# One-core hybrid decoder layer: five waits and small stages moved inside the head turn

## The chip, the cores and the metric

One core of one Trainium2 chip runs the whole kernel in one launch. The metric is device time in microseconds, the median of the timed runs; lower is better. A separate, profiled execution gives the trace from which all rows below are copied. Engines in the rows: PE is TensorE's matmuls, PEld its weight loads, DVE is VectorE, ACT is ScalarE, POOL is GpSimd, SP the engine whose queue starts the DMAs.

## The reference, cut to what matters

A decoder layer on 512 tokens of width 1024. The change lies in the first part, in which eight attention heads and eight heads of a gated delta rule run side by side from one input projection.

```python
h = rmsnorm(x, attn_norm[i])
proj = h @ w_in[i]
qa, ka, va, qb, kb, vb, zb, bb, ab, gl = jnp.split(proj, cuts, axis=-1)
...
# attention head: softmax pairs, w = probs0 - lam * probs1, oa = w @ va
oa = (rmsnorm(oa, subln_a[i]) * (1.0 - lam_init))
...
# delta head: short convolution and silu, then unit norm of q and k
qkv = jax.nn.silu(causal_dwconv(jnp.concatenate([qb, kb, vb], axis=-1), conv_b[i]))
qb = l2norm(qb) * (DK_B ** -0.5)
kb = l2norm(kb)
...
def step(state, inp):                     # once for each chunk
    v_new = u_c - w_c @ state
    o = (q_c * jnp.exp(g_c)[..., None]) @ state + a_c @ v_new
    state = state * jnp.exp(g_last)[..., None, None] + jnp.swapaxes(k_dec, -1, -2) @ v_new
    return state, o
...
ob = rmsnorm(ob, onorm_b[i]) * jax.nn.silu(zb)
```

After it come the branch gates and projections, an output projection, a gated MLP with a convolution, and a gated per-layer embedding. The change touches none of these.

## The kernel before, in words

Every engine has a program of its own, written out by hand. An engine runs its instructions in the order in which they stand, and `wait_ge` on a semaphore holds it and all that is queued behind. Sequences lie along the free axis: a head's tensor is 128 x 512 (`T`), cut into four chunks of 128 tokens (`NT`).

**Projections.** Each projection is one 128-column slice of the weights times the normalized input: eight steps of three matmuls of 512 columns (line 488: high by high, high by low part, low part by high) into one of banks 0 to 3. SP loads a slice into one of four slots, POOL rounds it (`w_hi`, line 438) and makes the remainder (`w_lo`, line 424, four pieces), and PE multiplies.

**Turns.** The function `turn(h, ...)` exists once for each engine. Turn h computes the delta rule of head h, the attention and the convolutions of head a = h + 1, and projects what is needed next: in turns 0 to 5 the seven slices qb, kb, vb, zb, qa, ka, va. Turn -1 has no delta rule, turn 6 (`STEPS_LATE`) has four slices to project, and turn 7 has no attention. The changed places lie in turns -1 to 6. On PE the projection steps (`f.step(n)`) are dealt out between the small matmuls of the chain, to cover its waits; how many go where stands in `STEPS`.

**Levels.** For n = 1 to 6, PE multiplies (line 668), ACT copies the result to `ui` (1036), PE multiplies again (678, 680), and DVE updates `xi` and `xt` (1435, 1437); `make_ct` (1370) prepares the masked matrix `ct` of the next level. Side work rides along: `maxima(a, 3)` (1308, 1313) for the softmax; `decay_beta` (1392), which multiplies `dec` by the beta rows that lie in bank 6; `finish_silu` (1354). `b_sum` (609) on PE sums the squares of q, then of k, into bank 6, which `decay_beta` must have read before; `b_r` on ACT (Ln at 867, Exp at 868) turns each sum into a norm. Its Ln signals `b_ln`: bank 6 has been read.

**Scan.** For chunk t = 0 to 3: a product with the state (724) and the state part of the output into bank 6 (726), from t = 1 on; DVE's copy of `us` (1479, 1483, semaphore `vnew`); the state's increment into bank 5 (735, `kv`); the output's second part into bank 6 (736); and DVE's update of `state` (1489, 1491). Around t = 0 stands `attend` (599), which makes head a's output in bank 3. ACT squares it (1080, `oa_sq`) and PE sums the squares into bank 4 (744, `oa_sum`), from which comes the output's norm. ACT's `silu_exp(a, 2)` (992, 967, 968) is the sigmoid of the convolved v (`b_sigmoid2`). `gate_z` (1001, 1006, 967, 968) copies z out of its bank and makes its sigmoid (`z_sigmoid`); DVE multiplies the two in `finish_z` (1515). DVE's side work in the scan is a list from which two entries are taken at each t: one after the copy of `us`, one after the update of the state.

Of the kernel before, what the change touches and what calls it, by code (L numbers as in the profile page):

```python
# [156 lines left out]
def build(nc, x, p, w_in, attn_norm, qnorm_a, knorm_a, lam_a, subln_a, rel_bias, conv_b, a_log_b,  # L157
# [4 lines left out]
    with ctx:  # L162
# [5 lines left out]
        def sem(name):  # L168
            if name not in sems:
                sems[name] = ctx.enter_context(nc.semaphore(name))  # L170
            return sems[name]
# [61 lines left out]
        qb, kb, vb, zb = (sb(n, [P, T], F32, ws) for n in ("qb", "kb", "vb", "zb"))  # L233
# [238 lines left out]
        def _(pe):  # L472
# [147 lines left out]
            def turn(h, at, fill, delta=True, attention=True, more_a=True, steps=STEPS):  # L620

                a = h + 1
# [96 lines left out]
                for t in range(NT):  # L719
                    ts = slice(t * P, (t + 1) * P)  # L720
                    if delta and t > 0:
                        pe.wait_ge(sem("state"), h * 3 + t)

                        pe.matmul(tiles(7)[:, t, :], wt_[:, t, :], state[:, :], start=False, stop=True,
                                  skip_group_check=True).then_inc(sem("ws"), 1)
                        pe.matmul(bank[6][:, ts], state[:, :], qeg[:, t, :], start=True, stop=False, skip_group_check=True)
                    f.step(scan[1 + t][0])
                    if delta:
                        pe.wait_ge(sem("vnew"), h * NT + (t + 1))
                        if t == 0:  # L730
                            pe.wait_ge(sem("w_copied"), h + 1)
                            if attention:
                                pe.wait_ge(sem("b_ln"), a * 2 + 2)
                        if t < NT - 1:
                            pe.matmul(bank[5][:, 0:P], kdec[:, t, :], us[:, t, :], start=True, stop=True).then_inc(sem("kv"), 1)
                        mm = pe.matmul(bank[6][:, ts], us[:, t, :], at_[:, t, :], start=(t == 0), stop=True, skip_group_check=True)
                        if t == NT - 1:
                            mm.then_inc(sem("ob_mm"), 1)
                    f.step(scan[1 + t][1])
                    if t == 0 and attention:  # L740
                        attend(a)
                    if t == 1 and attention:
                        pe.wait_ge(sem("oa_sq"), a + 1)
                        pe.matmul(bank[4][:, :], ones, pr[1][:, :], start=True, stop=True).then_inc(sem("oa_sum"), 1)  # L744
                for n, name in enumerate(("qa", "ka")):
# [110 lines left out]
        def _(act):  # L856
# [3 lines left out]
            def done(ins, name, value):  # L860

                ins.then_inc(sem(name) if isinstance(name, str) else name, 1)
                act.wait_ge(sem(name) if isinstance(name, str) else name, value)
# [89 lines left out]
            def keep_w(h, i):  # L953
                act.wait_ge(sem("a_turned"), h * 4 + (i + 1) + 1)
                done(nc.scalar.activation(wT[:, 0:i + 1, i * P:(i + 1) * P], tiles(3)[:, 0:i + 1, :], ACT.Copy),  # L955
                     "a_wT", h * 4 + (i + 1))
# [60 lines left out]
            def turn(h, at, delta=True, attention=True, more_a=True):  # L1017

                a = h + 1
                if not attention:  # L1020

                    act.wait_ge(sem("oa_done"), H + 1)
                    for k in range(H):
                        done(nc.scalar.activation(oa_hi[:, k, :], o_a[:, k, :], ACT.Copy), "o_high", k + 1)
                if attention:
                    softmax(a, 0)
                if h > 0:
                    ob_r(h - 1)
                if attention:
                    keep_w(a, 0)  # L1030
                    first_tap(a, 0, at("qb"))
                    softmax(a, 1)
                for n in range(1, NL):
                    if delta:
                        act.wait_ge(sem("level_u"), h * (NL - 1) + n)
                        done(nc.scalar.activation(ui[:, :, :], tiles(7), ACT.Copy), "ui", h * (NL - 1) + n)  # L1036
                    if attention:
                        if n == 2:
                            keep_w(a, 1)
                            silu_exp(a, 0)  # L1040
                        if n == 3:
                            softmax(a, 2)
                            first_tap(a, 1, at("kb"))
                            act.wait_ge(sem("g_rows"), a + 1)
                            if delta:
                                act.wait_ge(sem("qeg"), h + 1)
                            nc.scalar.activation(egl[:, a % 2, :, :], tiles(6)[:, :, P - 1:P], ACT.Exp)
                            done(nc.scalar.activation(eg[:, :, :].rearrange("p t c -> p (t c)"), bank[6][:, :], ACT.Exp),
                                 "eg", a + 1)
                            square_b(a, 0)  # L1050
                        if n == 4:
                            act.wait_ge(sem("g_rows_read"), a + 1)
                            done(nc.scalar.activation(dec[:, :, :], dec[:, :, :], ACT.Exp), "dec", a + 1)
                            keep_w(a, 2)
                        if n == 5:
                            silu_exp(a, 1)
                            softmax(a, 3)
                            b_r(a, 0)
                        if n == 6:
                            square_b(a, 1)  # L1060
                            first_tap(a, 2, at("vb"))
                    if n in (1, 3) and not attention:
                        gate_a(n // 2)
                    if n == 2 and not attention:
                        gate_z(h, at("zb"), attention)
                if delta:
                    act.wait_ge(sem("w_mm"), h + 1)
                    done(nc.scalar.activation(wt_[:, :, :], tiles(5), ACT.Copy, scale=-1.0), "w_copied", h + 1)
                if not attention:
                    gate_a(2)  # L1070
                    gate_a(3)
                if attention:
                    keep_w(a, 3)
                    v_copy(a)
                    b_r(a, 1)
                    if delta and more_a:
                        gate_z(h, at("zb"), attention)
                    silu_exp(a, 2)
                    act.wait_ge(sem("a_out"), a + 1)
                    done(nc.scalar.activation(pr[1][:, :], bank[3][:, :], ACT.Square), "oa_sq", a + 1)  # L1080
                    if more_a:
                        prep_qk(h + 2, 0, at("qa"))
                    act.wait_ge(sem("oa_sum"), a + 1)
                    rsqrt(pr[1][:, :], bank[4][:, :], 1.0 / P, ("oa_ln", "oa_r"), a + 1)
                    if not more_a:
                        gate_z(h, at("zb"), attention)
                if more_a:
                    prep_r(h + 2, 0, at("qa"))
                    prep_qk(h + 2, 1, at("ka"))
                if delta:  # L1090
                    act.wait_ge(sem("ob_mm"), h + 1)
                    if h > 0:
                        act.wait_ge(sem("ob_done"), h + 1)
                    done(nc.scalar.activation(sqo[:, :], bank[6][:, :], ACT.Square), "ob_sq", h + 1)
                if more_a:
                    prep_r(h + 2, 1, at("ka"))
                    prep_v(h + 2, at("va"))
# [11 lines left out]
            def b_r(h, n):  # L1109
                act.wait_ge(sem("b_sum"), h * 2 + (n + 1))  # L1110
                rsqrt(sqb[n][:, :], bank[6][:, :], 1.0, ("b_ln", "b_r"), h * 2 + (n + 1))
# [90 lines left out]
        def _(dve):  # L1202
# [195 lines left out]
            def turn(h, at, delta=True, attention=True, more_a=True):  # L1398

                a = h + 1  # L1400
# [27 lines left out]
                for n in range(1, NL):  # L1428
# [27 lines left out]
                    if n == 4 and attention:  # L1456
                        steps(conv(a, 1, at("kb")))
                        maxima(a, 3)
                    if n == 5 and attention:
                        decay_beta(a)  # L1460
                        steps(finish_silu(a, 1))
                        combine(a, 3)
                    if n == 6 and attention:
# [6 lines left out]
                side = []  # L1470
                if attention:
                    side = conv(a, 2, at("vb")) + [lambda: scale_qk(a, 1)]
                if delta and (more_a or not attention):
                    side = side + [lambda: finish_z(h)]
                if attention:
                    side = side + finish_silu(a, 2)
                if delta:
                    dve.wait_ge(sem("u_mm"), h + 1)
                    done(V.tensor_copy(us[:, 0, :], tiles(7)[:, 0, :]), "vnew", h * NT + 1)
# [221 lines left out]
```

## Time and profile before

| | |
|---|---|
| time, median of 3 | 1396.91 us (1396.87 to 1397.35) |
| the profiled execution's own time | 1394.66 us |
| its span, first to last instruction | 1392.6 us |
| mean granted TensorE clock in it | 0.99 |
| PE busy | 1305.9 us, 94% of the span |
| DVE, ACT, POOL busy | 724.6, 523.3, 642.4 us |
| PE waits for `oa_sq` at line 744, by the list of waits | 14.7 us, 7 times |
| PE waits for `decb` at line 609 | 9.5 us, 8 times |
| PE waits for `b_ln` at line 735 | 7.4 us, 7 times |

Busy shares are averages over the whole span. The change is about single waits, so the rows below follow one turn. A row of a timeline gives start, duration, engine, line, operation and tiles, the count of merged instructions, and in brackets the idle time of the engine just before with what ended it. A matmul's printed duration overlaps its successor's start: dense matmuls of 512 columns start 0.23 us apart though each is printed with 0.39 or 0.40.

### The profile page before, as it was taken

What the parts mean: (1) busy time and instruction counts of PE and PEld (TensorE: products, weight loads), DVE (VectorE), ACT (ScalarE), POOL (GpSimd) and SP (SyncE); (2) the same over time, 40 slices, a digit from 0 to 9 for tenths busy, and PEclk for the clock granted to TensorE, in tenths of its full rate; (3) what the DMA queues carried; (4) which work ended last, traced back from release to release, by engine and by line L of the source; (5) the groups of instructions that cost most, each with busy time, mean ns of one, the idle gap of its engine ahead of it and who ended that gap; (6) DMA issues with size and microseconds to landing.
All of it is one profiled execution on the core that took longest, in us unless ns stands there. A gap on an engine that the chain in (4) does not pass through costs nothing.

```text
span 1392.6 us, 19271 instructions
## 1 busy us (share of the span) xinstructions
PE 1305.9 (94%) x6453; PEld 1044.9 (75%) x6453; DVE 724.6 (52%) x1137; ACT 523.3 (38%) x811; POOL 642.4 (46%) x757
## 2 busy tenths in 40 slices
PE   4889999898999989899899999999999999999998
PEld 3657768676777867677688888877887778878776
DVE  3264748375473836547452113215888871781634
ACT  4353444435344453534423322345332221221252
POOL 2434243242424335242253646436666775666533
PEclk9999999999999999999999999999999999999999
DMA  6412111111111111111122335222333224233222
GB/s 187 120 46 60 32 49 43 46 50 42 47 45 46 46 37 55 46 46 31 34 63 56 106 88 168 76 76 76 105 91 91 87 87 127 60 91 110 68 75 80
DMA packets 188128, 100.71 MB, mean 72 GB/s; under 512 B 3654, under 2 KB 186905, under 8 KB 188057
## 3 DMA queue, kind: packets, MB, share of 16 engines
q1 hardware_dynamic: 188057, 99.79, 25.0%
q8 instruction: 41, 0.67, 0.2%
q14 instruction: 30, 0.25, 0.1%
HBM read 97.67 MB, written 2.11 MB: 72 GB/s over the span
## 4 chain that ended last, share of the span: by engine, by line
PE 51%; POOL 19%; issue 17%; DVE 6%; ACT 5%; SPq 1%; DMA 0%; POOLq 0%; DVEq 0%; ACTq 0%
PE bank L488 30%; POOL w_lo L424 19%; PE bank L680 3%; PE bank L668 3%; PE bank L678 2%; PE bank L585 1%; PE bank L609 1%; PE bank L599 1%; PE bank L565 1%; PE bank L744 1%; PE bank L631 1%; PE bank L592 1%; ACT pr L949 1%; DVE ast L1313 1%; PE bank L640 1%
## 5 line engine op out<-in xcount | busy, mean ns | idle before, releaser
L424 POOL TENSOR_TENSOR w_lo<-w_raw,w_hi 128x256 fp32r<-128x256 f32 x692 | 576.4, 867 | 302.1 <-ACT w_hi L876 297.2
L488 PE MATMUL bank<-hn_hi,w_hi 128*128 128x512 f32 x1000 | 423.5, 424 | 9.3 <-POOL w_lo L424 9.3
L488 PE MATMUL bank<-hn_hi,w_lo 128*128 128x512 f32 x1000 | 393.5, 394 | 0.0
L488 PE MATMUL bank<-hn_lo,w_hi 128*128 128x512 f32 x1000 | 392.6, 393 | 0.0
L438 POOL CAST w_hi<-w_raw 128x1024 fp32r<-128x1024 f32 x61 | 65.8, 1079 | 431.6 <-PE bank L488 431.6
L488 PEld LDWEIGHTS bank<-hn_hi,w_hi 128*128 128x128 f32 x1000 | 190.1, 190 | 54.7 <-issue 19.5
L488 PEld LDWEIGHTS bank<-hn_hi,w_lo 128*128 128x128 f32 x1000 | 189.2, 189 | 41.3
L488 PEld LDWEIGHTS bank<-hn_lo,w_hi 128*128 128x128 f32 x1000 | 190.3, 190 | 37.7 <-issue 6.7
L876 ACT ACTIVATE w_hi<-w_raw 128x1024 fp32r<-128x1024 f32 x120 | 127.4, 1062 | 109.3 <-PE bank L488 95.2
L1600 DVE SCALAR_TENSOR_TENSOR u<-vr,pt,u 128x511 f32<-128x511 f32 x88 | 75.1, 853 | 12.9 <-DVE u L1598 1.2
L1174 ACT ACTIVATE s<-u 128x512 f32<-128x512 f32 x22 | 13.9, 633 | 178.7 <-DVEq L1603 178.7
L488 PE MATMUL bank<-fa_hi,w_hi 128*128 128x512 f32 x176 | 71.3, 405 | 2.2 <-POOL w_lo L424 2.2
L488 PE MATMUL bank<-fa_hi,w_lo 128*128 128x512 f32 x176 | 68.6, 390 | 0.0
L488 PE MATMUL bank<-fa_lo,w_hi 128*128 128x512 f32 x176 | 68.6, 390 | 0.0
L1036 ACT ACTIVATE ui<-bank 128x512 f32<-128x512 f32 x48 | 28.8, 599 | 83.7 <-PE bank L668 83.0
L668 PEld LDWEIGHTS bank<-xi,ct 128*128 128x128 f32 x384 | 48.9, 194 | 9.9 <-issue 8.0
L668 PE MATMUL bank<-xi,ct 128*128 128x128 f32 x384 | 52.5, 280 | 0.9 <-DVE xi L1435 0.9
L1370 DVE TENSOR_TENSOR ct<-lt,sq 128x512 f32<-128x512 f32 x56 | 51.3, 916 | 2.8 <-DVE qb L1343 0.2
L680 PE MATMUL bank<-xt,ui 128*128 128x64 f32 x384 | 50.9, 275 | 0.0
L680 PEld LDWEIGHTS bank<-xt,ui 128*128 128x128 f32 x384 | 46.8, 192 | 1.9 <-ACT ui L1036 1.7
L678 PEld LDWEIGHTS bank<-ui,xt 128*128 128x128 f32 x320 | 40.9, 191 | 9.7 <-ACT ui L1036 7.3
L955 ACT ACTIVATE wT<-bank 128x128 f32<-128x128 f32 (+3 forms) x32 | 14.0, 438 | 87.1 <-PE bank L592 87.1
(259 smaller groups left out, 1882.8 us busy)
## 6 DMA issues: line engine op xcount, KB each, us to landing
w_raw<-in_w_in SPq DMA_DIRECT2D x73, 512.0 KB, 3.8
w_raw<-in_w_up SPq DMA_DIRECT2D x44, 512.0 KB, 3.8
w_raw<-in_w_down SPq DMA_DIRECT2D x16, 512.0 KB, 4.0
w_raw<-in_w_br_a SPq DMA_DIRECT2D x8, 512.0 KB, 4.1
w_raw<-in_w_br_b SPq DMA_DIRECT2D x8, 512.0 KB, 4.0
w_raw<-in_w_out SPq DMA_DIRECT2D x8, 512.0 KB, 4.0
w_raw<-in_w_ple_gate SPq DMA_DIRECT2D x8, 512.0 KB, 4.1
w_raw<-in_w_down SPq DMA_DIRECT2D x8, 384.0 KB, 3.4
```

The source lines that it names most:

```text
L424: ins = pool.tensor_tensor(wlo[c.slot][:, ks, :], raw[c.slot][:, ks, :], whi[c.slot][:, ks, :].bitcast(F32), ALU.subtract)
L438: pool.tensor_copy(whi[c.slot][:, :, :], raw[c.slot][:, :, :]).then_inc(high_ready, 1)
L488: mm = pe.matmul(acc, w[c.slot][:, i, :], xx[:, x0 + i, :], start=(i == 0 and n == 0), stop=last)
L565: pe.matmul(bank[c.bank][:, :], half, sqr[n][:, :], start=True, stop=True).then_inc(sem("a_sum"), 1)
L668: mm = pe.matmul(tiles(7)[:, t, :], ct[n % 2][:, t, :], xi[:, t, :], start=True, stop=True)
L678: pe.matmul(packed(5, n, 0, t), xt[:, t, :], lane(ui[:, t, :], n, 0), start=True, stop=True)
L680: mm = pe.matmul(packed(5, n, 1, t), ui[:, t, :], lane(xt[:, t, :], n, 1), start=True, stop=True)
L876: done(nc.scalar.activation(whi[c.slot][:, :, :], raw[c.slot][:, :, :], ACT.Copy), high_ready, c.number + 1)
L955: done(nc.scalar.activation(wT[:, 0:i + 1, i * P:(i + 1) * P], tiles(3)[:, 0:i + 1, :], ACT.Copy), "a_wT", h * 4 + (i + 1))
L1036: done(nc.scalar.activation(ui[:, :, :], tiles(7), ACT.Copy), "ui", h * (NL - 1) + n)
L1370: done(V.tensor_tensor(ct[n % 2][:, :, :], lt[:, :, :], level_mask(n), ALU.mult), "ct", h * NL + (n + 1))
L1600: link(V.scalar_tensor_tensor(out=u[:, back:], in0=vr[:, 0:T - back], scalar=tap(j), in1=u[:, back:], op0=ALU.mult, op1=ALU.add))
```

## The change

No operation is added or taken away, and no size changes. Six places are edited:

- PE, scan at t = 0: the wait for `b_ln` moves from ahead of the state's increment (735 before, 733 after) to behind it, where line 736 is the first to write bank 6.
- PE: the sum of squares of the attention output (744) moves from behind t = 1 to behind t = 2.
- ACT: `b_r(a, 1)`, k's norm, moves ahead of `keep_w(a, 3)` and `v_copy(a)`.
- ACT: `gate_z` moves from ahead of `silu_exp(a, 2)` to behind the square `oa_sq` (turns 0 to 5).
- DVE: `decay_beta(a)` moves from level 5 to level 4, behind `maxima(a, 3)`; in turns with a delta rule it thereby stands ahead of `make_ct` and the updates of level 5.
- DVE: `finish_silu(a, 2)` and `finish_z(h)` change places in the side list.

```diff
@@ PE, scan @@
                         if t == 0:
                             pe.wait_ge(sem("w_copied"), h + 1)
-                            if attention:
-                                pe.wait_ge(sem("b_ln"), a * 2 + 2)
                         if t < NT - 1:
                             pe.matmul(bank[5][:, 0:P], kdec[:, t, :], us[:, t, :], start=True, stop=True).then_inc(sem("kv"), 1)
+                        if t == 0 and attention:
+                            pe.wait_ge(sem("b_ln"), a * 2 + 2)
                         mm = pe.matmul(bank[6][:, ts], us[:, t, :], at_[:, t, :], start=(t == 0), stop=True, skip_group_check=True)
...
-                    if t == 1 and attention:
+                    if t == 2 and attention:
                         pe.wait_ge(sem("oa_sq"), a + 1)
                         pe.matmul(bank[4][:, :], ones, pr[1][:, :], start=True, stop=True).then_inc(sem("oa_sum"), 1)
@@ ACT @@
                 if attention:
+                    b_r(a, 1)
                     keep_w(a, 3)
                     v_copy(a)
-                    b_r(a, 1)
-                    if delta and more_a:
-                        gate_z(h, at("zb"), attention)
                     silu_exp(a, 2)
                     act.wait_ge(sem("a_out"), a + 1)
                     done(nc.scalar.activation(pr[1][:, :], bank[3][:, :], ACT.Square), "oa_sq", a + 1)
+                    if delta and more_a:
+                        gate_z(h, at("zb"), attention)
@@ DVE @@
                     if n == 4 and attention:
                         steps(conv(a, 1, at("kb")))
                         maxima(a, 3)
+                        decay_beta(a)
                     if n == 5 and attention:
-                        decay_beta(a)
                         steps(finish_silu(a, 1))
...
+                if attention:
+                    side = side + finish_silu(a, 2)
                 if delta and (more_a or not attention):
                     side = side + [lambda: finish_z(h)]
-                if attention:
-                    side = side + finish_silu(a, 2)
```

What stands on ACT behind the levels of turn 0 (`ui` is not shown; `silu0` takes v, `silu1` takes z; a - row is of before, a + row of after):

```order
+L867 ACTIVATE sqb1<-bank6,sm 128x512 [waits b_sum,w_copied]
+L868 ACTIVATE sqb1<-sqb1 128x512 [waits b_ln]
+L955 ACTIVATE wT<-bank3 128x4x128 [waits a_turned,b_r]
 L919 ACTIVATE va<-bank4 128x512 [waits va_T,a_wT]
-L867 ACTIVATE sqb1<-bank6,sm 128x512 [waits b_sum,va_ready]
-L868 ACTIVATE sqb1<-sqb1 128x512 [waits b_ln]
-L1001 ACTIVATE zb<-bank1 128x512 [waits product,b_r]
+L992 ACTIVATE silu0<-vb 128x512 [waits b_silu,b_conv2,va_ready]
+L967 ACTIVATE silu0<-silu0,sm 128x512 [waits scalar_step]
+L968 ACTIVATE silu0<-silu0 128x512 [waits scalar_step]
+L1078 ACTIVATE pr1<-bank3 128x512 [waits a_out,b_sigmoid2]
+L1001 ACTIVATE zb<-bank1 128x512 [waits product,oa_sq]
```

The norm now stands ahead of the two copies, and z's copy (its exponential, logarithm and exponential follow it) behind the square of the attention output, where before it stood ahead of v's sigmoid.

On DVE, in the same turn, the end of the side work in the scan, from chunk t = 2 on (`vbt` is the memory of `us`):

```order
 L1483 COPY vbt<-bank 128x128 [waits ws,qkb_ready]
-L1515 TENSOR_TENSOR zb<-zb,silu 128x512 [waits z_sigmoid,vnew]
-L1491 SCALAR_TENSOR_TENSOR state<-state,egl,bank 128x128 [waits kv,zb_ready]
-L1354 TENSOR_TENSOR vb<-vb,silu 128x512 [waits b_sigmoid2,state]
-L1483 COPY vbt<-bank 128x128 [waits ws,vb_ready]
+L1354 TENSOR_TENSOR vb<-vb,silu 128x512 [waits b_sigmoid2,vnew]
+L1491 SCALAR_TENSOR_TENSOR state<-state,egl,bank 128x128 [waits kv,vb_ready]
+L1515 TENSOR_TENSOR zb<-zb,silu 128x512 [waits z_sigmoid,state]
+L1483 COPY vbt<-bank 128x128 [waits ws,zb_ready]
 L1499 SCALAR_TENSOR_TENSOR o_a<-bank,sm,pr 128x512 [waits oa_r,vnew]
```

The product with z now stands directly ahead of the last copy of `us`, and v's product ahead of the last update of the state.

On DVE, levels 4 and 5 of the same turn:

```order
 L1313 TENSOR_REDUCE ast<-bank 128x1 [waits a_exp,vector_step]
 L1313 TENSOR_REDUCE ast<-bank 128x1
-L1370 TENSOR_TENSOR ct<-lt,sq 128x512 [waits a_nmax]
+L1392 TENSOR_TENSOR decb<-dec,bank 128x512 [waits b_rows,dec,a_nmax]
+L1370 TENSOR_TENSOR ct<-lt,sq 128x512 [waits decb]
 L1435 TENSOR_TENSOR xi<-xi,bank 128x8x32 [waits level_vt,ct]
 L1437 TENSOR_TENSOR xt<-xt,bank 128x8x32 [waits xi]
-L1392 TENSOR_TENSOR decb<-dec,bank 128x512 [waits b_rows,dec,xt]
-L1354 TENSOR_TENSOR kb<-kb,silu 128x512 [waits b_sigmoid1,decb]
+L1354 TENSOR_TENSOR kb<-kb,silu 128x512 [waits b_sigmoid1,xt]
```

`decb` now stands ahead of `ct` and of the two updates instead of behind them.

## Rows read from the trace of the kernel before

**Rows 1.** The page, its first line.

```profile
span 1392.6 us, 19271 instructions
```

**Rows 2.** Waits, whole span: who waited for whom, us in total, times, longest.

```profile
PE bank L744 <- ACT pr L1080: 14.7, 7, 2.7
...
PE bank L609 <- DVE decb L1392: 9.5, 8, 1.8
...
PE bank L735 <- ACT sqb L867: 7.4, 7, 1.1
```

**Rows 3.** Windows: stretch, us, each engine's busy time, granted clock, DMA share, GB/s.

```profile
244.89:326.16 81.27, 76.61 (x432) 60.66 (x433) 47.35 (x87) 36.68 (x68) 29.40 (x36) 1.00 0.17 46
326.16:409.05 82.89, 78.25 (x433) 61.60 (x433) 47.04 (x87) 36.69 (x68) 30.04 (x36) 0.98 0.17 45
...
346.40:349.90 3.50, 3.50 (x8) 2.30 (x9) 0.91 (x2) 0.00 (x0) 0.00 (x0) 0.51 0.02 5
```

**Rows 4.** Timeline of PE in turn 1, pieces from level 6 on.

```profile
243.16 0.39 PE L488 MATMUL bank<-hn_lo,w_hi 128*128 128x512 f32 x1
243.39 0.40 PE L488 MATMUL bank<-hn_hi,w_lo 128*128 128x512 f32 x1
244.89 1.10 PE L609 MATMUL bank<-sqb,sq 128*128 128x512 f32 x2 [1.10 <-DVE decb L1392]
...
257.32 0.46 PE L735 MATMUL bank<-vbt,kdec 128*128 128x128 f32 x2 [1.06 <-ACT sqb L867]
...
265.12 1.12 PE L744 MATMUL bank<-pr,sq 128*128 128x512 f32 x2 [2.00 <-ACT pr L1080]
266.08 0.39 PE L724 MATMUL bank<-state,ui 128*128 128x128 f32 x2
...
268.36 0.38 PE L724 MATMUL bank<-state,ui 128*128 128x128 f32 x2
...
269.50 0.38 PE L736 MATMUL bank<-at_,vbt 128*128 128x128 f32 x2
```

**Rows 5.** Timeline of ACT in the scan of turn 1.

```profile
257.87 0.60 ACT L1001 ACTIVATE zb<-bank 128x512 f32<-128x512 f32 x1
...
259.74 0.63 ACT L968 ACTIVATE silu<-silu 128x512 f32<-128x512 f32 x1
262.39 0.63 ACT L992 ACTIVATE silu<-vb 128x512 f32<-128x512 f32 x1 [2.02 <-DVEq L1345]
...
264.47 0.60 ACT L1080 ACTIVATE pr<-bank 128x512 f32<-128x512 f32 x1
```

**Rows 6.** Timeline of DVE in turn 1, levels 4 and 5, then the scan.

```profile
241.20 1.14 DVE L1370 TENSOR_TENSOR ct<-lt,sq 128x512 f32<-128x512 f32 x1
243.15 0.42 DVE L1435 TENSOR_TENSOR xi<-xi,bank 128x256 f32<-128x256 f32 x1 [0.81 <-PE bank L680]
...
244.06 0.69 DVE L1392 TENSOR_TENSOR decb<-dec,bank 128x512 f32<-128x512 f32 x1
...
266.90 0.69 DVE L1515 TENSOR_TENSOR zb<-zb,silu 128x512 f32<-128x512 f32 x1
...
268.85 0.29 DVE L1483 COPY vbt<-bank 128x128 f32<-128x128 f32 x1
```

**Rows 7.** Line 1515 over the whole run: durations in ns, min/median/max.

```profile
L1515 DVE TENSOR_TENSOR zb<-zb,silu x8: 691/692/1240, 185.7 to 739.8; 128x512 f32<-128x512 f32 x8
```

**Rows 8.** Timeline of POOL behind the scan of turn 1.

```profile
270.72 1.04 POOL L438 CAST w_hi<-w_raw 128x1024 fp32r<-128x1024 f32 x1 [11.97 <-PE bank L488]
```

**Rows 9.** Timeline of PE in turn 6.

```profile
653.28 1.65 PE L609 MATMUL bank<-sqb,sq 128*128 128x512 f32 x2 [1.85 <-DVE decb L1392]
...
672.96 1.12 PE L744 MATMUL bank<-pr,sq 128*128 128x512 f32 x2 [2.69 <-ACT pr L1080]
```

**Rows 10.** Windows of turn 6 behind those two waits, columns as in Rows 3.

```profile
653.28:657.10 3.82, 3.82 (x12) 2.87 (x13) 2.04 (x4) 1.68 (x3) 0.00 (x0) 0.55 0.02 4
...
672.96:678.49 5.53, 5.45 (x21) 4.26 (x22) 1.94 (x5) 1.32 (x2) 0.00 (x0) 0.69 0.00 0
```

## The prediction

> **What bounds the kernel now.** I read the list of waits first, then windows over single turns, then the timeline of each engine in one turn. In turn 1, from one sum of q's squares to the next, PE is busy 76.61 of 81.27 us [rows 3], so PE is the engine that sets the pace of a turn, and a turn gets shorter only by what PE stops waiting. The list of waits has three waits of PE that the change aims at: 14.7 us for the square of the attention output, 9.5 for `decb`, 7.4 for k's norm [rows 2]. In turn 1 they are 2.00, 1.10 and 1.06 us [rows 4]; turns 0 to 5 repeat these three within 0.01 us, and turn 6 has 2.69, 1.85 and 1.06 [rows 2, 9].
>
> The printed idle time is a little less than the loss. Dense matmuls start 0.23 us apart (243.16, 243.39), and line 609 starts 1.50 behind the last of them, so this wait costs 1.27 against 1.10 printed [rows 4]. I add the same 0.16 or so to the others: 1.22 for k's norm and 2.16 for the square. Together 4.65 us in a turn.
>
> The clock is a cost of its own. Behind the 2.00 us stall of turn 2 the granted clock was 0.51 in a window of 3.50 us, the lower of the two levels (1.2 against 2.4 GHz), and that turn took 82.89 us where turn 1 took 81.27: 1.62 us for one fall [rows 3]. Two of the six 2.00 us stalls were followed by a fall (turns 2 and 5), as were the 1.85 and 2.69 us stalls of turn 6 (granted 0.55 and 0.69 behind them, [rows 10]); none of the stalls of 1.0 to 1.1 us was.
>
> **Part by part, in a turn of 0 to 5, by the times of turn 1.** Nothing is added, so no work term appears; it is all order.
>
> *decay times beta, level 4.* `decb` takes 0.69 us and would run from 241.20 to 241.9, where `ct` started before [rows 6]. Its inputs are made earlier in the level, and PE has not asked for bank 6 by then. PE's line 609 then goes at 243.62: 1.27 saved. What becomes late is `ct` and with it `xi`: `ct` took 1.14 us, so it would end at about 243.1 instead of 242.3, and `xi` waits for PE until 243.15 anyway [rows 6]. Even 0.6 us of lateness in `xi` is covered, since the sum of squares occupies PE for 0.96 us (as line 744 does from 265.12 to 266.08, [rows 4]) between PE's arrival and the next level's product. I cost it at nothing; without that cover it would be up to 0.4.
>
> *k's norm.* ACT has been free since it copied `w`, and the sum was made long before the scan, so the Ln that frees bank 6 runs well before it is wanted; besides, the increment no longer waits for it. Saved: 1.22. The two copies that now stand behind the norm wait for PE's transposes anyway and keep their place.
>
> PE reaches the scan's first increment 1.27 + 1.22 = 2.49 earlier, at 254.83. The chain behind it (state, convolution of v, sigmoid of v, square) hangs on that increment: v's first exponential starts at 262.39 - 2.49 = 259.90 and the square is ready at 264.47 + 0.60 - 2.49 = 262.58 [rows 4, 5].
>
> *The sum, one chunk later.* PE would arrive at the old place 2.00 + 0.16 before the square. The new place is one chunk behind, which is 268.36 - 266.08 = 2.28 us of PE work [rows 4]. That is 0.12 more than the wait: the 2.16 are saved, with next to nothing to spare.
>
> *z's gate, and the new wait.* This is the one place where the change makes something late. `gate_z` took 257.87 to 260.37 = 2.50 us, in time that ACT had free; now it starts behind the square, at about 262.6, and ends at 265.12 [rows 5]. DVE's product with z (0.69) starts 0.1 behind that, and the last copy of `us` (0.29) is queued behind it: 265.2 + 0.69 + 0.03 + 0.29 = 266.2 [rows 6]. PE takes the result 0.15 later (`decb` ends at 244.75, line 609 starts at 244.89, [rows 4, 6]), so the last product with `us` (736) starts at 266.35. Without this wait PE would be there at 269.50 - 2.49 - 2.16 = 264.85 [rows 4]. **New stall: 1.50 us.** PE holds everything behind it, the projections too. The trace of before has no such wait. Its bounds: nothing if z were early after all, 2.05 if the product takes its longest 1.24 us [rows 7]. I take 1.50, since the product's median is 0.69 [rows 7] and each other part is a row too.
>
> Here the Trainium skill speaks against the change. Its page "SBUF — State Buffer", section "SBUF: two separate sides", says that VectorE and GpSimd share a port pair which one of them holds for a whole instruction, and that a VectorE operation with two SBUF inputs is among those that it blocks. The product with z has two such inputs, so by that rule the product waits wherever a GpSimd piece is under way.
>
> What the rows say of it: the product took between 0.69 and 1.24 us [rows 7]. With 1.24 in each of the six turns the sum would be 3.3 smaller and the time 1370.2. POOL stood idle 11.97 us before its cast at 270.72, thus through the scan from 258.75 on, waiting for PE [rows 8]; even moved 3 us earlier, that stretch covers the product, so I keep 0.69.
>
> *v's sigmoid before z.* It is ready at 264.44 - 2.49 = 261.95, its product and the state's update fit ahead of 263.7, when PE has finished line 744. Nothing.
>
> Net in a turn: 1.27 + 1.22 + 2.16 - 1.50 = 3.15; six turns 18.9.
>
> *Falls of the clock.* Turns 2 and 5 lose their fall at the square: 2 x 1.62 = 3.2. A stall of 1.50 is between those that never brought a fall (1.1) and those that did (1.85, and 2.00 in two of six); I take none.
>
> *Turn 6.* No z here in the scan. `decb`: 1.85 + 0.16, of which I take off 0.3, an estimate, since the next steps then meet ACT still busy with the softmax: 1.7. k's norm 1.2. The square: 2.69 + 0.16 = 2.85, but a chunk of this turn has one projection step fewer (three dense matmuls, 0.70), thus 2.28 - 0.70 = 1.58 of cover, so 1.27 stay: 1.6 saved. Two falls [rows 10]: 3.2. Together 7.7.
>
> *Turn -1.* It has no delta rule; `decb` stands where it stood relative to the other work, and PE waits about 0.2 for the square, which goes. 0.2.
>
> Sum: 18.9 + 3.2 + 7.7 + 0.2 = 30.0. The profiled execution's own time is 1394.66 (span 1392.6, [rows 1]), 2.25 below the median shown. So 1364.7 for a profiled execution, and 1366.9 for the median. The weights can follow: the POOL row shows that it waits for PE, not PE for it [rows 8].
>
> **Rivals.**
>
> *The new stall starts falls of the clock.* For it: 1.50 us is nearer to 1.85 than 1.06 is, and the stall follows other short pauses. Against: seven stalls of 1.06 and eight up to 1.85 brought one fall. Two to six falls cost 3.2 to 9.7: 1370 to 1377. Chance 0.14.
>
> *z costs nothing.* If ACT or PE were 1.5 us off in my favour, for instance if PE meets a further wait of its own in chunk 2 that z hides behind: six turns gain 1.50 more, 1357.9. Against: the z chain is 5.2 us of ACT behind v's convolution, and every part is a row [rows 5]. Chance 0.06.
>
> *A moved stage is late somewhere else.* The sum has 0.12 us to spare only, `xi` some 0.5. If another wait takes the place of the `decb` or of the square's wait (1 to 2 us in a turn), six turns give back 6 to 12: 1373 to 1379, 1382 at the worst. Chance 0.10.
>
> *POOL meets z's product.* Each product takes 1.24: 1370.2, as worked out above. Chance 0.04.
>
> *Hidden anyway.* If PE's lead is only spent waiting for weights, the time stays. Against: [rows 8], and no wait for weights shows in turns 0 to 5. 1396.9. Chance 0.02.
>
> *Slower: the z chain holds the scan.* The same place, line 736 at t = 3, behind ACT's gate and DVE's product. The stall must be longer than 1.50 + 30.0 / 6 = 6.5 us for the time to rise. That needs ACT to start the gate 5 us later than I have it, say behind a projection that is not finished. Before, `gate_z` ran at 257.87 without waiting for its projection, which speaks against it [rows 5]. At 8 us: 1396.9 + 6 x 1.5 = 1406. Chance 0.03.
>
> **How the numbers follow.** The forecast has 0.61, with its own range 1362 to 1371 (product with z at 1.24 in most turns: up to +3.3; 0.12 us of spare missed by 0.3: +1.8; new stall 1 us shorter in each turn: about -5). Adding z at no cost at the lower end and falls or another wait at the upper end, 1359 to 1377 leaves out less than 2 in 10. A time within 0.2% (2.8 us) of before is all that this kernel's measurement cannot tell from no change; of the cases only the hidden one ends there, 0.02 and 0.01 more for mixtures. Slower has 0.03, faster 0.94.
>
> **What the profile after would show.** PE's wait at line 609 for `decb`, at the first increment (then line 733) for ACT's norm, and at 744 for the square are gone in turns 0 to 5; 744 keeps about 1.1 in turn 6. A new wait of PE at line 736 for DVE's copy, 1.3 to 1.5 us printed, in each of turns 0 to 5, with DVE at 1515 waiting for ACT's 968. The turn from one line 609 to the next takes 78.1 us. Half-clock windows behind 744 are gone. Wrong would be: another releaser in front of 668 or 744, a stall at 736 over 2 us or absent, or falls behind it.

## The result and the profile after

The changed kernel takes 1364.62 us (median of 4, 1363.99 to 1365.4) against 1396.89 for the kernel before in the same runs: a ratio of 0.9772 with a 95% interval of 0.9755 to 0.9789. The forecast was 1366.9 in a range of 1359 to 1377. The profiled execution took 1363.99 us by its own time, 30.67 less than that of before; the sum had said 30.0.

The waits of the changed kernel, whole span (columns as in [rows 2]):

```profile
DVE zb L1515 <- ACT silu L968: 15.7, 7, 3.2
...
PE bank L736 <- DVE vbt L1483: 8.3, 6, 1.4
```

Of the three waits of [rows 2] one is left, once: 0.47 us at line 744 in turn 6. PE has one new wait that is long, six times, at the place and with the releaser that were forecast. Turn 1 on PE, to be read against [rows 4]:

```profile
240.06 0.39 PE L488 MATMUL bank<-hn_hi,w_lo 128*128 128x512 f32 x1
240.28 0.59 PE L609 MATMUL bank<-sqb,sq 128*128 128x512 f32 x1
...
251.17 0.39 PE L488 MATMUL bank<-hn_hi,w_lo 128*128 128x512 f32 x1
251.40 0.27 PE L733 MATMUL bank<-vbt,kdec 128*128 128x128 f32 x1
...
259.01 0.40 PE L488 MATMUL bank<-hn_hi,w_lo 128*128 128x512 f32 x1
259.25 1.02 PE L744 MATMUL bank<-pr,sq 128*128 128x512 f32 x2
...
261.02 0.40 PE L488 MATMUL bank<-hn_hi,w_lo 128*128 128x512 f32 x1
262.80 0.49 PE L736 MATMUL bank<-at_,vbt 128*128 128x128 f32 x2 [1.38 <-DVE vbt L1483]
```

Lines 609, 733 and 744 each start 0.22 to 0.24 us behind the matmul before them, which is the dense distance: nothing is waited for. The last product with `us` starts 1.78 behind. ACT and DVE show why ([rows 5, 6] before; line 1078 is 1080 of before):

```profile
256.40 0.63 ACT L992 ACTIVATE silu<-vb 128x512 f32<-128x512 f32 x1 [4.64 <-DVEq L1345]
...
258.49 0.60 ACT L1078 ACTIVATE pr<-bank 128x512 f32<-128x512 f32 x1
259.12 0.60 ACT L1001 ACTIVATE zb<-bank 128x512 f32<-128x512 f32 x1
...
260.99 0.63 ACT L968 ACTIVATE silu<-silu 128x512 f32<-128x512 f32 x1
```

```profile
261.73 0.69 DVE L1515 TENSOR_TENSOR zb<-zb,silu 128x512 f32<-128x512 f32 x1 [2.09 <-ACT silu L968]
262.45 0.29 DVE L1483 COPY vbt<-bank 128x128 f32<-128x128 f32 x1
```

The square is ready at 259.09, and PE takes it at 259.25 with nothing to spare, as worked out. z's gate then runs from 259.12 to 261.62, DVE multiplies at 261.73, and the copy that PE needs ends at 262.74. In front of the first of these rows ACT stood idle for 4.64 us. Experiment 3 uses that.

Windows of turns, from one turn's last line 736 to the next, first of the kernel before and then of the changed kernel (columns as in [rows 3]; the third row of each is turn 6):

```profile
188.29:269.50 81.21, 76.55 (x434) 60.64 (x433) 47.63 (x86) 36.69 (x68) 29.41 (x35) 1.00 0.17 46
269.50:352.42 82.92, 78.26 (x434) 61.65 (x433) 47.35 (x86) 36.69 (x68) 29.42 (x35) 0.98 0.17 45
597.69:678.49 80.80, 73.73 (x407) 58.54 (x406) 45.97 (x86) 35.55 (x66) 26.27 (x30) 0.96 0.14 40
```

```profile
184.86:262.80 77.94, 76.05 (x433) 60.68 (x433) 47.96 (x86) 36.67 (x68) 29.97 (x35) 1.00 0.18 48
262.80:340.88 78.08, 76.19 (x433) 60.70 (x433) 47.67 (x86) 36.68 (x68) 29.96 (x35) 1.00 0.18 48
574.76:647.85 73.09, 70.86 (x406) 56.11 (x406) 45.46 (x85) 35.09 (x66) 26.24 (x30) 1.00 0.16 44
```

A turn is 3.2 us shorter (81.21 to about 77.97, five of them between 77.94 and 78.08). In turn 1 PE's work is the same to 0.5 us, so what went is waiting; the longer busy times in the second and third rows of before come with a lower granted clock (0.98 and 0.96). In turns 0 to 6 of the changed kernel the granted clock stayed at the upper level.

### The profile page after: what moved, and what is told of

Read it like the earlier page. It is cut to its first block, busy times and chain, and to the rows that moved or that the text cites. A ratio compares the mean times of both kernels' runs of the same rounds, so it can differ in the third digit from the quotient of the medians.

```text
span 1362.2 us, 19271 instructions
## 1 busy us (share of the span) xinstructions
PE 1299.9 (95%) x6453; PEld 1043.6 (77%) x6453; DVE 726.8 (53%) x1137; ACT 523.2 (38%) x811; POOL 644.1 (47%) x757
## 4 chain that ended last, share of the span: by engine, by line
PE 51%; POOL 20%; issue 17%; DVE 5%; ACT 5%; SPq 1%; DMA 0%; POOLq 0%; DVEq 0%; ACTq 0%
PE bank L488 31%; POOL w_lo L424 20%; PE bank L680 3%; PE bank L668 3%; PE bank L678 2%; PE bank L585 1%; PE bank L599 1%; PE bank L609 1%; PE bank L565 1%; ACT silu L967 1%; ACT silu L968 1%; PE bank L592 1%; PE bank L613 1%; ACT pr L949 1%; PE bank L631 1%
## 5 line engine op out<-in xcount | busy, mean ns | idle before, releaser
L949 ACT ACTIVATE pr<-bank,ast 128x128 f32<-128x128 f32 (+3 forms) x64 | 33.8, 528 | 29.6 <-DVE ast L1313 28.3
```

The costliest lines, as they stand in the source:

```text
L949: done(nc.scalar.activation(pr[j][:, 0:w], bank[3 + j][:, 0:w], ACT.Exp, bias=ast[:, 2 + j:3 + j], scale=-1.0, accum_out=ast[:, 4 + j:5 + j]),
```

## The experiments

Eight kernels, each timed in turns with the kernel before on the same chip. The first four share a median of before of 1395.53 us, the last four one of 1395.19.

**1. decay times beta alone.** The kernel before with

```diff
                         maxima(a, 3)
+                        decay_beta(a)
                     if n == 5 and attention:
-                        decay_beta(a)
```

> The kernel before with one edit: decay times beta at level 4. My theory (each wait of TensorE is on the path, and the lateness of ct is covered): PE's wait at line 609 for decb goes, 1.27 us in each of turns 0 to 5 and 1.7 us in turn 6, together 9.3 us less than before, about 1387.5. Rival (the moved product makes ct and xi late, and the wait only changes its place to line 668): no change, 1397. In the profile: no releaser decb in front of 609; under my theory nothing in its place in front of 668.

Measured: 1387.52, ratio 0.9944 (0.9931 to 0.9958), 8.0 us less where 9.3 were expected. No wait for `decb` is left, and no new wait at 668 took its place. Its turns 1 and 4:

```profile
189.71:271.20 81.49, 77.93 (x434) 61.89 (x432) 47.90 (x86) 36.70 (x68) 29.96 (x35) 0.98 0.17 46
434.24:514.13 79.89, 76.31 (x433) 60.72 (x432) 47.94 (x86) 36.70 (x68) 29.97 (x35) 1.00 0.17 47
```

The lower row is a turn without a fall: 1.32 less than 81.21. But the upper kind stands in five of six turns (0 to 5) of this execution, where the kernel before had two: the 2.00 us wait for the square is still there, and in this execution the clock falls behind it more often (turn 6 has one fall, where before had two). Part of the gain seems to be paid back so; experiment 2 has more on it.

**2. k's norm alone,** both edits: `b_r(a, 1)` ahead of the copies, and the wait for `b_ln` behind the increment.

> The kernel before with two edits: k's norm ahead of the two copies on ACT, and the wait for b_ln behind the state's increment on PE. My theory: 1.22 us in each of turns 0 to 6, 8.5 us less than before, about 1388.4, with the wait for the square at line 744 unchanged at 2.00 us, since its whole chain moves with the increment. Rival (the time goes into the wait for the square): the wait at 744 grows to 3.2 us and the time stays at 1397.

Measured: 1390.17, ratio 0.9965 (0.9951 to 0.9978), 5.4 us less, between the two theories. The wait at 744 did not grow (14.7 us in total, 2.0 each), so the rival's mechanism is out. The clock fell again in five of the turns 0 to 5:

```profile
190.51:272.06 81.55, 77.94 (x434) 61.94 (x433) 47.02 (x86) 36.67 (x68) 30.02 (x35) 0.98 0.17 46
353.65:433.58 79.93, 76.33 (x434) 60.71 (x433) 47.62 (x86) 36.67 (x68) 29.41 (x35) 1.00 0.17 47
```

Without a fall the turn is 1.28 shorter, about what the sum had (1.22). That is three falls more than before has in these turns and one fewer in turn 6, thus two more, at 1.6 each 3.2 us: what is missing. The timed executions bear it out. Their mean granted clock is on record: 0.982 to 0.986 here (median 0.985) and 0.985 to 0.987 in experiment 1, against 0.987 to 0.990 (median 0.988) of the kernel before. One fall, 3.50 us at 0.51 [rows 3], takes about 0.0012 off the mean (an estimate: 0.49 x 3.50 / 1392.6), so the medians stand for two to three more falls here.

**3. The changed kernel with z's gate back in its old place.**

```diff
                     b_r(a, 1)
                     keep_w(a, 3)
                     v_copy(a)
+                    if delta and more_a:
+                        gate_z(h, at("zb"), attention)
                     silu_exp(a, 2)
...
-                    if delta and more_a:
-                        gate_z(h, at("zb"), attention)
```

> The changed kernel with one edit undone: z's gate on ACT stands ahead of v's sigmoid again, DVE's order stays as changed. My theory (the new stall in front of line 736 is z's chain and nothing else; ACT is free from 251.8 to 256.4 in turn 1, which holds the gate's 2.5 us, and z's projection is finished at 250.0): the stall of 1.38 us printed goes in all six turns, 1.55 us each, 9.3 us less than the changed kernel, about 1355.3. Rival (the gate then delays v's sigmoid and the square, which is why it was moved): a wait for the square of 1 to 2.5 us comes back in front of 744, and the time is 1365 to 1375.

Measured: 1354.35, ratio 0.9704 (0.9691 to 0.9718), 41.2 us less than before, and about 9.5 less than the changed kernel by the two ratios. The window of its turn 1, then ACT and PE in it:

```profile
184.40:260.73 76.33, 75.82 (x433) 60.75 (x432) 47.93 (x86) 36.71 (x68) 29.96 (x35) 1.00 0.18 49
```

```profile
251.27 0.60 ACT L1001 ACTIVATE zb<-bank 128x512 f32<-128x512 f32 x1
...
253.14 0.63 ACT L968 ACTIVATE silu<-silu 128x512 f32<-128x512 f32 x1
255.88 0.63 ACT L992 ACTIVATE silu<-vb 128x512 f32<-128x512 f32 x1 [2.10 <-DVEq L1345]
```

```profile
258.73 1.02 PE L744 MATMUL bank<-pr,sq 128*128 128x512 f32 x2
...
260.73 0.38 PE L736 MATMUL bank<-at_,vbt 128*128 128x128 f32 x2
```

The turn is 1.64 shorter than the 77.97 of the changed kernel. The gate fits into ACT's idle time with 2.10 us left over. v's sigmoid starts as early in the turn as in the changed kernel (71.48 us behind the window's start, there 71.54), and neither 744 nor 736 has a wait. The rival falls: moving the gate bought nothing and cost the new stall.

**4. The changed kernel with the sum of squares behind chunk 1 again** (`if t == 1 and attention:`).

> The changed kernel with one edit undone: the sum of the output's squares stands behind chunk 1 again. My theory (the two waits lie one behind the other in the same scan, so they overlap): PE waits 2.0 us for the square at 744 again, and the stall at 736 for z is gone, since PE arrives there 0.6 us behind z. Net 0.6 us in each of six turns and 1.3 in turn 6, 4.9 us, plus 1.6 us for each fall of the clock that the 2.0 us stalls bring back (0 to 3): 1370 to 1374. Rival (the two add up): 2.16 in each of six turns, 14.6 us with turn 6, about 1379.

Measured: 1373.3, ratio 0.984 (0.9824 to 0.9855), 0.7% above the changed kernel. Its PE in turn 1, and the windows of turns 1 and 2:

```profile
258.71 1.12 PE L744 MATMUL bank<-pr,sq 128*128 128x512 f32 x2 [2.00 <-ACT pr L1078]
...
263.08 0.38 PE L736 MATMUL bank<-at_,vbt 128*128 128x128 f32 x2
```

```profile
184.50:263.08 78.58, 76.09 (x434) 60.78 (x433) 47.95 (x86) 36.67 (x68) 29.98 (x35) 1.00 0.17 48
263.08:343.32 80.24, 77.73 (x434) 62.07 (x433) 47.64 (x86) 36.68 (x68) 29.97 (x35) 0.98 0.17 47
```

The 2.00 us wait is back, the stall at 736 is gone, and the turn is 78.58: 0.6 above 77.97, not 2.16. The two waits lie one behind the other and do not add. The rest of the difference is one fall in turns 0 to 5 (1.6 us) and turn 6, which took 76.53 us here against 73.09, with another fall.

**5. Only PE's wait moved.** The kernel before with the wait for `b_ln` behind the increment, ACT untouched.

> The kernel before with one edit: the wait for b_ln stands behind the state's increment on PE; ACT's order is as before. My theory: the increment starts 1.2 us earlier, but PE then waits for the same Ln in front of line 736, about 0.9 us, and all that follows on PE stands where it stood: no change, 1395 to 1397. Rival (the increment is what the chain hangs on, so its start alone matters): the 8 us of both edits together, about 1388 to 1390.

Measured: 1395.01, ratio 1.0 (0.9991 to 1.0009). PE in its turn 1:

```profile
257.53 0.39 PE L733 MATMUL bank<-vbt,kdec 128*128 128x128 f32 x2
258.66 0.49 PE L736 MATMUL bank<-at_,vbt 128*128 128x128 f32 x2 [0.74 <-ACT sqb L867]
```

The increment runs 1.2 us earlier in the turn (67.81 us behind the last line 736 of turn 0, at 189.72, against 257.32 - 188.29 = 69.03 before), and the same Ln holds PE one instruction later. A turn without a fall takes 81.00 against 81.21, so 0.2 is gained, but the clock fell in three of turns 0 to 5 instead of two. The rival, 8 us, falls.

**6. Only k's norm ahead of the copies.** `b_r(a, 1)` moved on ACT; PE's wait as before.

> The kernel before with one edit: k's norm ahead of the two copies on ACT; PE still waits for b_ln in front of the increment. My theory: the norm is finished about 3 us before PE asks, so this edit alone gives all that the two gave together, about 1390. Rival (both edits are needed): 1393 or more. In the profile: no PE wait for L867 in front of 735.

Measured: 1390.28, ratio 0.9966 (0.9956 to 0.9976), the same as experiment 2. The norm's order is the whole effect; it had five falls too.

**7. The changed kernel with decay times beta back at level 5.**

> The changed kernel with one edit undone: decay times beta at level 5 again. My theory: the wait at 609 comes back with its 1.27 us in each of turns 0 to 5 and 1.7 in turn 6, 9.3 us more than the changed kernel, 1374, with the stall at 736 unchanged at 1.38 us. Rival (z's chain does not move with PE's earlier wait, so the stall at 736 shrinks by as much): no more than 1366.

Measured: 1375.5, ratio 0.9861 (0.9846 to 0.9877). That is 0.9% or 12 us above the changed kernel by the two ratios, where 9.3 was expected. The profiled turns agree with the step: 79.31 us against 77.97, 1.34 each, and turn 6 takes 74.78 against 73.09, 1.69 more; together 9.7. The stall at 736 kept its 1.38, so the waits did not hide each other. Most of what remains is turn 0, in which the clock fell at the start, as it did in the kernel before and not in the changed kernel:

```profile
121.46:187.75 66.29, 63.23 (x374) 50.90 (x374) 42.51 (x82) 27.74 (x54) 19.24 (x24) 0.97 0.15 41
```

That is 3.03 more than the changed kernel's 63.26, of which 1.34 are the step and 1.7 the fall; with it the profiled spans differ by 11.4 us (1373.6 against 1362.2). The last 1 us up to the 12 is within the two intervals.

**8. Three edits alone.** The kernel before with decay times beta at level 4, k's norm ahead of the copies, and `if t == 2 and attention:`. z's gate, DVE's list and PE's wait stay as they were.

> The kernel before with three edits alone: decay times beta at level 4, k's norm ahead of the two copies, the sum of squares behind chunk 2. z's gate, DVE's side list and PE's wait for b_ln stay as before. My theory: the other three edits are not needed, so this equals the changed kernel with the gate back in its old place, 1354.4, with turns of 76.3 us. Rival (DVE's old order, with v's product behind the last state update, holds back the last copy of us): 1 us or more in each turn, above 1360.

Measured: 1353.57, ratio 0.9711 (0.9698 to 0.9725); the ratio does not differ from that of experiment 3. Its turns 1 and 2:

```profile
183.21:259.53 76.32, 75.82 (x433) 60.77 (x432) 47.97 (x86) 36.70 (x68) 30.02 (x35) 1.00 0.18 49
259.53:335.93 76.40, 75.89 (x433) 60.81 (x432) 47.67 (x86) 36.69 (x68) 30.00 (x35) 1.00 0.18 49
```

PE is busy 75.82 of 76.32 us. Three of the six edits give everything. PE's wait and DVE's list give nothing beside them, and z's gate takes about 1.6 us in each turn. DVE's old list together with the late gate was not run, so what the list is worth there is not shown.

## Why the prediction was right, point by point

- **decay times beta, 1.27 in a turn, ct's lateness covered.** Right: 1.32 and 1.34 in experiments 1 and 7, no new wait at 668. DVE in turn 1 of the changed kernel:

```profile
237.86 0.69 DVE L1392 TENSOR_TENSOR decb<-dec,bank 128x512 f32<-128x512 f32 x1
238.59 1.22 DVE L1370 TENSOR_TENSOR ct<-lt,sq 128x512 f32<-128x512 f32 x1
239.84 0.42 DVE L1435 TENSOR_TENSOR xi<-xi,bank 128x256 f32<-128x256 f32 x1
```

  `xi` no longer waits for PE, as in [rows 6], but for `ct`: that cover is used up, and the sum of squares on PE, which runs meanwhile, hides the little lateness.
- **k's norm, 1.22.** Right: 1.28 in turns without a fall. The text gave both edits the credit; experiments 5 and 6 show that ACT's order is all of it.
- **The sum one chunk later, 2.16 saved with 0.12 to spare.** Right in the changed order: 744 starts at the dense distance. As a part on its own it is worth 0.6 there (experiment 4), since without it z's stall would be hidden.
- **The new stall, 1.50.** Its size was right: the gap of 1.78 behind the last matmul is 1.55 over the dense 0.23, 1.38 or 1.39 as printed, in each of six turns. The releaser and place were those named, and experiment 3 ties it to the gate's place alone.
- **The port that DVE shares with POOL.** It cost nothing in z's product, which took 0.69 us while POOL was idle. But `ct` above took 1.22, and POOL was at work on a weight slice:

```profile
237.41 1.04 POOL L438 CAST w_hi<-w_raw 128x1024 fp32r<-128x1024 f32 x1 [10.61 <-PE bank L488]
238.53 3.70 POOL L424 TENSOR_TENSOR w_lo<-w_raw,w_hi 128x256 fp32r<-128x256 f32 x4
```

  In the changed kernel's turns 0 to 5 every `ct` during which a piece of line 424 was under way took 0.74 to 1.24 us, and every other one 0.69; in turn 6 one `ct` took 0.69 in spite of such a piece (at 601.77). `decb`, with one input in PSUM, took 0.69 beside the cast of line 438. That is what the Trainium skill says on its page "SBUF — State Buffer", section "SBUF: two separate sides" (a VectorE operation with two SBUF inputs waits for one of GpSimd that reads SBUF): the trace agrees, but for that one `ct`. The text looked for the collision at z's product; it is at `ct`, where the cover was just large enough.
- **Falls of the clock.** Right in size (82.92 against 81.21, 1.7), and in that the stall of 1.38 us brings none: none in twelve such stalls (changed kernel and experiment 7). The sum had four falls, two at the square and two in turn 6. A fifth fall of before, at the start of turn 0, was not in it. The window of turn 0 to its last line 736 fell from 68.22 to 63.26 us, 5.0 where the other turns fell by 3.2, and its granted clock rose from 0.97 to 1.00 (before, then changed):

```profile
120.07:188.29 68.22, 63.56 (x373) 51.13 (x374) 42.46 (x81) 27.74 (x54) 19.17 (x24) 0.97 0.14 39
```

```profile
121.60:184.86 63.26, 61.38 (x373) 49.82 (x373) 42.80 (x81) 27.73 (x54) 19.73 (x24) 1.00 0.16 42
```

  That this fall went is luck. In all ten profiled executions PE waits 1.77 us for `ka` at line 585 there, whatever the edits, and in seven the clock fell behind it, those of experiments 3, 7 and 8 among them.
- **Turn 6, 7.7.** Measured 80.80 - 73.09 = 7.71, but that it agrees so well is luck too. The time in which PE was not busy fell by 7.07 - 2.23 = 4.84, where the sum had 1.7 + 1.2 + 1.6 = 4.5, and PE's busy time by 73.73 - 70.86 = 2.87, where it had 3.2 for the two falls. The wait for the square kept 0.47 us and not about 1.1, and there is a new short wait for the state's update at line 724:

```profile
643.42 0.49 PE L724 MATMUL bank<-state,ui 128*128 128x128 f32 x2 [0.37 <-DVE state L1491]
645.74 1.12 PE L744 MATMUL bank<-pr,sq 128*128 128x512 f32 x2 [0.47 <-ACT pr L1078]
```

- **Turn -1, 0.2.** Too small to be seen beside what the clock did there (next point).
- **Sum.** From the start of turn 0 to the end of turn 6's scan the trace lost 558.42 - 526.25 = 32.17 us (120.07 to 678.49 before, 121.60 to 647.85 after). That is six times 3.24, three falls, and turn 6. The span shrank by only 30.4 of it, since the profiled execution came to turn 0 1.5 us later than that of before. Up to there PE was busy 90.32 us at a granted clock of 0.93, where before it was busy 87.32 at 0.96:

```profile
0.00:120.07 120.07, 87.32 (x353) 62.12 (x353) 47.31 (x91) 54.99 (x97) 47.35 (x64) 0.96 0.38 111
```

```profile
0.00:121.60 121.60, 90.32 (x353) 64.84 (x354) 46.68 (x91) 54.95 (x97) 47.24 (x64) 0.93 0.38 110
```

  So 1.7 us of luck at the start of turn 0 and 1.5 the other way ahead of it nearly cancel, and 30.67 lies closer to the forecast 30.0 than the account behind it can claim. The medians differ by 32.3.
- **Hidden by the weights.** No: in experiment 8 turns of 76.3 us are still 99% busy on PE.

## What to carry to other kernels

Where one engine sets the pace, add up its single waits in one turn of the loop and ask of each what it hangs on; moving the producer into idle time of its own engine (k's norm) paid 1.28 us a turn, while moving the waiter by one instruction gave 0.2. Before moving a stage out of the way of another, look whether it is in the way: z's gate was not even in the way in the kernel before, where ACT stood idle for 2.02 us behind it [rows 5], and moving it cost 1.6 us a turn. Waits in one chain need not add, so take each edit out of the finished version as well as adding it alone.

## What the runs showed of the hardware that was not expected

Behind the same 2.00 us wait of PE the granted clock fell, by one profiled execution of each kernel, in 2 of 6 turns before, in 3 of 6 in experiment 5, in 5 of 6 in experiments 1, 2 and 6, and in 1 of 6 in experiment 4, each fall for about 1.6 us of time (81.55 against 79.93). The wait was the same in all; the length of the turns and where in them PE paused otherwise differed, and which of these decides is not shown. The timed executions of experiments 1, 2 and 6 had a lower mean clock than the kernel before too (medians 0.987, 0.985 and 0.985 against 0.988). So a saving of 1.2 us in a turn can be eaten in part by falls that come with it (5.4 us were left of the 8.5 expected in experiment 2), as long as the long wait itself is there. With the 2.00 us wait gone, and 1.38 or 1.39 the longest wait in turns 1 to 5, no fall was left in these turns of any of the four kernels (changed, and experiments 3, 7 and 8).
